# Token, norm, tap, subkey and bias layouts made by the host, and a first dense tile fed in quarters

## What is computed

```python
xn = rmsnorm(x, norm1_w)              # x * rsqrt(mean(x*x) + eps) * w
proj = xn @ w_in                      # 1024 -> 3088 columns; 16 of them feed a gate
log_a = log_sigmoid(gr @ gla_w_alpha + gla_b_alpha) / 16
...
s = einsum('thpd,hpkd->thpk', q, subkeys)      # product keys, top 16 of each half
...
u = h @ w_up; u = conv3(u, taps) + bias        # per channel, causal
h = h + sigmoid(rmsnorm(h) @ w_gate) * (p @ w_proj)   # side input p, two layers
...
logits = q . k * scale + rel_bias[bucket(t - s)]      # -inf outside the band of 128
```

## Time and profile before

| | us |
|---|---|
| median of 3 runs | 1544.4 |
| lowest, highest | 1544.03, 1548.16 |
| the profiled execution, its time | 1549.62 |
| the profiled execution, its span | 1547.8 |
| PE busy | 1387.3 (90%) |
| DVE busy | 1032.8 (67%) |
| ACT busy | 707.7 (46%) |
| POOL busy | 622.3 (40%) |

### The profile page before, as it was taken

How to read it: one execution, slowest core, us unless ns; L and a number is a source line. 1 busy time by engine, 2 the same in 40 slices (tenths; PEclk the granted TensorE clock), 3 DMA queues, 4 the chain that set the end, 5 groups by cost and what they waited for, 6 DMA issues and landing times.

```text
span 1547.8 us, 18260 instructions
## 1 busy us (share of the span) xinstructions
PE 1387.3 (90%) x5985; PEld 971.1 (63%) x5985; DVE 1032.8 (67%) x1923; ACT 707.7 (46%) x1374; POOL 622.3 (40%) x581
## 2 busy tenths in 40 slices
PE   7989979777787877787779999999999999999998
PEld 6877964333333333233335879788888788888887
DVE  5895787666666666666663548569863586498733
ACT  5534633233322333333334373477654745776534
POOL 2330777433333433333362521045442612364414
PEclk9999989999999999989999999899999999999999
DMA  9286699999999999999999500557665443476650
GB/s 319 82 143 224 217 333 411 421 422 421 422 423 421 421 422 422 422 421 422 422 413 348 200 29 35 164 163 210 196 211 178 159 142 108 121 207 194 216 193 28
DMA packets 187077, 415.00 MB, mean 268 GB/s; under 512 B 9883, under 2 KB 113923, under 8 KB 160387
## 3 DMA queue, kind: packets, MB, share of 16 engines
q0 software_dynamic: 43776, 268.45, 42.3%
q1 hardware_dynamic: 143090, 145.66, 30.6%
q10 hardware_dynamic: 144, 0.04, 0.0%
HBM read 409.93 MB, written 4.19 MB: 268 GB/s over the span
## 4 chain that ended last, share of the span: by engine, by line
PE 51%; DMA 21%; DVE 9%; POOL 7%; ACT 6%; issue 5%; ACTq 0%; POOLq 0%; DVEq 0%
DMA expert_rows<-in_peer_uv,route_idx 15%; PE ps L2548 10%; PE ps L2379 9%; PE ps L2092 7%; PE ps L2094 7%; PE ps L2093 7%; DMA scratch<-in_peer_uv,route_idx 5%; PE ps L2549 5%; DVE weights_lo L443 2%; POOL weights_lo L591 2%; POOL expert_rows L642 2%; ACT weights_hi L436 1%; POOL expert_rows L674 1%; PE ps L2057 1%; POOL expert_rows L661 1%
## 5 line engine op out<-in xcount | busy, mean ns | idle before, releaser
L1672 DVE CUSTOM_DVE_ANT_0 expert_rows<-expert_rows,ps 128x1024 f32<-128x1024 f32 x184 | 224.1, 1220 | 142.6 <-DMA expert_rows<-in_peer_uv,route_idx 131.6
L591 POOL TENSOR_TENSOR weights_lo<-weights_raw,weights_hi 128x512 fp32r<-128x512 f32 x120 | 159.6, 1366 | 374.5 <-ACT weights_hi L436 332.5
L2379 PE MATMUL ps<-expert_rows,scratch 128*128 128x512 f32 x512 | 241.9, 629 | 58.3 <-ACT scratch L981 58.3
L674 POOL DMA_INDIRECT expert_rows<-in_peer_uv,route_idx x156 | 148.3, 951 | 229.7 <-PE ps L2379 193.4
L436 ACT CAST weights_hi<-weights_raw 128x2048 fp32r<-128x2048 f32 x98 | 185.5, 1917 | 105.5 <-PE ps L2094 80.3
L2379 PEld LDWEIGHTS ps<-expert_rows,scratch 128*128 128x128 f32 x512 | 100.6, 201 | 198.6 <-issue 118.9
L2548 PE MATMUL ps<-x_normT,weights_hi 128*128 128x512 f32 x640 | 222.5, 393 | 0.0
L443 DVE TENSOR_TENSOR weights_lo<-weights_raw,weights_hi 128x2048 fp32r<-128x2048 f32 x68 | 160.5, 2366 | 74.4 <-ACT weights_hi L436 74.1
L967 ACT ACTIVATE proj<-proj 128x4 f32<-128x4 f32 x64 | 13.2, 206 | 402.1 <-DVE proj L1672 402.1
L2092 PE MATMUL ps<-weights_hi,x_normT 128*128 128x512 f32 (+1 forms) x496 | 188.1, 379 | 9.9 <-DVE weights_lo L443 4.2
L2094 PE MATMUL ps<-weights_hi,x_normT 128*128 128x512 f32 (+1 forms) x496 | 184.8, 372 | 0.0
(11 more groups left out here) (364 smaller groups left out, 2462.3 us busy)
## 6 DMA issues: line engine op xcount, KB each, us to landing
weights_raw<-in_ffn_up SPq DMA_DIRECT2D x88, 512.0 KB, 5.0
weights_raw<-in_ffn_down SPq DMA_DIRECT2D x22, 1024.0 KB, 4.9
weights_raw<-in_ab_w_in SPq DMA_DIRECT2D x14, 1024.0 KB, 5.7
weights_raw<-in_w_in SPq DMA_DIRECT2D x12, 1024.0 KB, 7.5
weights_raw<-in_ple_gate SPq DMA_DIRECT2D x8, 1024.0 KB, 6.2
weights_raw<-in_c_w_in SPq DMA_DIRECT2D x6, 1024.0 KB, 6.0
weights_raw<-in_w_out SPq DMA_DIRECT2D x4, 1024.0 KB, 12.7
weights_raw<-in_peer_w_query SPq DMA_DIRECT2D x4, 1024.0 KB, 12.4
```

The costliest lines, as they stand in the source:

```text
L591: ins = pool.tensor_tensor(w.lo[:, c], w.raw[:, c], w.hi[:, c].bitcast(F32), ALU.subtract)
L674: nc.gpsimd.indirect_dma_start(out=dst, out_offset=None, in_=table, in_offset=bass.IndirectOffsetOnAxis(ap=r_idx[:, q, n:n + 1], axis=0)). ...
L1672: ins = nc.vector.tensor_tensor_reduce(out=rows, in0=rows, in1=tokens, scale=1.0, scalar=0.0, op0=ALU.mult, op1=ALU.add, accum_out=r_dot[: ...
L2379: ins = pe.matmul(PS[:, (J[f"peer_{t}"] + m) % 8, :], DIAG[b][:, k, :], rows[:, m * BANK:(m + 1) * BANK], start=False, stop=False, skip_gr ...
```

## The change

- The host lays out x with the width on the partitions (`x_cols`), the six norm vectors as columns, taps and their bias as columns, the subkeys turned, the side input turned, and the banded bias in full (`window_bias`, 2 MB). The joined expert table was made by the host before, too.
- x in columns is loaded first, in two halves, then pieces 0 and 1, then x in rows. ACT and DVE make hi and lo of x from it, 8 instructions of 128x256 each.
- Pieces 0 and 1 are converted in quarters of 512 columns on ACT and DVE, and PE's first tile waits for each quarter by itself.
- The roots come behind these on ACT. The alpha job takes two banks. PE's turns, the eight spins, the conv and bias jobs, and the subkey and side-input jobs are gone from `PLAN`.
- One semaphore of the second block's gate is merged into another.

```diff
-PLAN = [("vecs", 1), ("norm0_0", 2), ("norm0_1", 2), ("win", 2), ("gr", 1), ("conv", 1), ("relb", 1),
-        ("win_1", 1), ("alpha", 1), ("win_1b", 1), ("win_2", 2), ...
+PLAN = [("win", 2), ("gr", 1),
+        ("win_1", 1), ("alpha", 2), ("win_1b", 1), ("win_2", 2), ...
...
+        "x_cols": inputs["x"][0].T.reshape(KC, P, S).transpose(1, 0, 2),
+        "vec_cols": np.concatenate([columns(n) for n in norms], 1),
+        "subkey_cols": inputs["peer_subkeys"][0].reshape(2 * PH, NKEYS, P).transpose(2, 0, 1),
+        "p_cols": inputs["p_2"][:, 0].transpose(0, 2, 1).reshape(2, 2, P, S).transpose(0, 2, 1, 3),
+        "window_bias": biases[rows].transpose(0, 2, 1),
...
@@ SP
-            sp.dma_start(C[:, 0:P], a["c_small"][:, 0:P]).then_inc(sem("ident_loaded"), 16)
-            for t in range(TT):
-                sp.dma_start(X[:, t, :], a["x"][0, t * P:(t + 1) * P, :]).then_inc(sem(f"x_loaded{t}"), 16)
+            for half in range(2):
+                cols = slice(4 * half, 4 * half + 4)
+                sp.dma_start(XCOLS[:, cols, :], a["x_cols"][:, cols, :]).then_inc(sem(f"x_cols_loaded{half}"), 16)
             for p in halves(0):
                 load("win", p)
+            for t in range(TT):
+                sp.dma_start(X[:, t, :], a["x"][0, t * P:(t + 1) * P, :]).then_inc(sem("x_loaded"), 16)
...
-            sp.wait_ge(evac_done, END["relb"])
-            sp.dma_start(bias_scratch.rearrange("h (t u) -> h t u", u=PER),
-                         BROW[:, 0:PER].unsqueeze(1).broadcast_to([SWH, P, PER])).then_inc(sem("bias_written"), 16)
...
-            sp.dma_start(SKN, a["peer_subkeys"][0].rearrange("h q k d -> k (h q) d")).then_inc(sem("subkeys_loaded"), 16)
-            sp.wait_ge(pe_done, END["subk_rest"])
...
+            sp.dma_start(BIAS, a["window_bias"]).then_inc(sem("bias_loaded"), 16)
@@ ACT
+            act.dma_start(VEC[:, :], a["vec_cols"]).then_inc(sem("vec_loaded"), 16)
...
+            for f in range(KC):
+                if f % 4 == 0:
+                    act.wait_ge(sem(f"x_cols_loaded{f // 4}"), 16)
+                nc.scalar.activation(XHI[:, f, :], XCOLS[:, f, :], ACT.Copy,
+                                     scale=VEC[:, NORM_COL[0] + f:NORM_COL[0] + f + 1]).then_inc(sem("first_hi"), 1)
+            for half in halves(0):
+                w = pieces["win", half]
+                act.wait_ge(raw_loaded[w.r], w.landed)
+                for c in range(4):
+                    cols = slice(c * BANK, (c + 1) * BANK)
+                    act.copy(w.hi[:, cols], w.raw[:, cols]).then_inc(hi_ready[w.h] if c == 3 else sem("first_hi"), 1)
             for t in range(TT):
-                norm_root(0, t, (sem(f"x_loaded{t}"), 16), (sem(f"x_loaded{t}"), 16))
-            act.wait_ge(evac_done, END["vecs"])
-            for half in range(2):
-                norm_hi(0, 0, (half,))
-                split("win", half)
-            norm_hi(0, 1)
+                norm_root(0, t, (sem("x_loaded"), 32), (sem("x_loaded"), 32))
@@ DVE
+            for half in halves(0):
+                w = pieces["win", half]
+                for c in range(4):
+                    cols = slice(c * BANK, (c + 1) * BANK)
+                    v.wait_ge(*((hi_ready[w.h], w.count) if c == 3 else (sem("first_hi"), KC + 3 * half + c + 1)))
+                    nc.vector.tensor_tensor(w.lo[:, cols], w.raw[:, cols], w.hi[:, cols].bitcast(F32),
+                                            ALU.subtract).then_inc(lo_ready[w.h] if c == 3 else sem("first_lo"), 1)
...
-            j = J["subk"]
-            freed(nc.vector.tensor_copy(SKT[:, 0:4, :], bank(j).rearrange("p (b t) -> p b t", b=4)), j)
@@ PE
-            for t in range(TT):
-                norm_T(0, t)
-            spin(J["win"], 8, P)
-            for t in range(TT):
-                dense_tile("win", 0, t, normed(0, t))
+            b = bank(tile_job("win", 0, 0))
+            for f in range(KC):
+                w, c = pieces["win", f // 4], f % 4
+                pe.wait_ge(*((lo_ready[w.h], w.count) if c == 3 else (sem("first_lo"), KC + 3 * (f // 4) + c + 1)))
+                hi, lo = part(w.hi, 4), part(w.lo, 4)
+                ins = product(b, xs(f, slice(0, P)), (hi[:, c, :], lo[:, c, :]), f == 0, f == KC - 1)
+            ins.then_inc(pe_done, 1)
+            dense_tile("win", 0, 1)
```

More of the change, by code:

```diff
@@ L1367, in _ @@
             v.wait_ge(sem("norm_rstd"), rstd_no[0])
-            for half in range(2):
-                norm_lo(0, 0, (half,))
-                split_lo(v, "win", half)
-            norm_lo(0, 1)
             v.wait_ge(sem("gr_hi_ready"), 1)
@@ L1377, in early_tables @@
                 freed(nc.vector.tensor_copy(GRT, bank(J["gr"])[0:GRANK, 0:S]), J["gr"])
-                freed(nc.vector.tensor_copy(CONV[:, :, :], bank(J["conv"])[:, 0:8 * 2 * FT].rearrange("p (l n) -> p l n", l=2)),
-                      J["conv"])
-                v.wait_ge(sem("rel_loaded"), 48)
-                freed(nc.vector.tensor_tensor(BROW, bank(J["relb"])[0:SWH, 0:384], OUTSIDE, ALU.add), J["relb"], wait=True)
                 v.wait_ge(sem("const_loaded"), 16)
@@ L2167, in _ @@
             ins.then_inc(pe_done, 1)
[L2168 to L2173 removed]
             dense_tile("win", 1, 0)
             pe.wait_ge(evac_done, END["gr"])
[L2176 removed]
             for t in range(TT):
[L2178 to L2179 removed]
+                pe.matmul(bank(J["alpha"] + t)[:, 0:256], GRT[:, t * P:(t + 1) * P], W_ALPHA,
+                          start=True, stop=True).then_inc(pe_done, 1)
             dense_tile("win", 1, 1)
@@ L2296, in _ @@
             spin(J["wout"], 3)
-            def subkeys(j, m):
-                pe.wait_ge(sem("subkeys_loaded"), 16)
-                transposes(j, [SKN[:, 4 * m + n, :] for n in range(4)])
             def head_tokens(t, j):
@@ L2319, in first_head @@
             def first_head():
-                subkeys(J["subk"], 0)
                 head_tokens(0, J["score_first"])
@@ L2329, in _ @@
             ins.then_inc(pe_done, 1)
-            for m in range(3):
-                subkeys(J["subk_rest"] + m, m + 1)
             head_tokens(1, J["query_0"])
```

127 lines of the change are left out of this document (48 added, 79 removed), and 4 rows, old and new, of the table PLAN.

## The result

| | us |
|---|---|
| kernel before, median of 22 runs | 1547.54 (1543.98 to 1552.63) |
| changed kernel, median of 22 runs | 1550.69 (1547.07 to 1555.46) |
| ratio of the two, 95% interval | 1.0020 (1.0012 to 1.0027) |
| profiled execution of the changed kernel: time, span | 1552.2, 1550.4 |

I had forecast 2.0 us less and measured about 3.1 us more. That lies inside the 0.3% that I had called no change, but its interval leaves out 1, and the forecast time and range are both missed. Of the 8.3 us between the forecast of 1542.4 and the 1550.7 measured, 3.1 are the starting point: I had counted from 1544.4, the median of three runs, and 22 runs gave 1547.5.

A forecast was written before the change was run, and what follows sets the result against it. The bound changes from stage to stage; at the start POOL's lo of piece 3 decides. The start's 2.0 us, all other edits zero, came off the median 1544.4: 1542.4 us, range 1537.5 to 1547.0.

The forecast's parts named there:

- The start sum: From first loads to the first `win_1` tile: done at 34.0 instead of 36.0 us, 2.0 us won.
- POOL's gap: Inside `win_1`, PE stands 2.4 us until POOL finishes the lo of piece 3 at 31.1 us.
- the cover behind it: Behind `win_1`: pieces 4 and 5 come no later, are wanted at 41 us, and the 2.0 us won stay.
- The subkeys' zero: At the subkey transposes: they are hidden in waits for DVE, so removing them wins zero.
- the covers gone: At the subkeys: 0.7 us instead of zero if the waits that hide the transposes and DVE's copy go.
- the rule on the clock: On PE: 1.2 GHz is the default and activity releases it; at the start real matmuls now pay for the warm-up.
- The side input's zero: At the side input's 4 transposes: PE waits 0.34 us for DVE anyway, so zero, at most 0.45 for each layer.
- the bias: Window bias transfers: no engine waits for them, so zero, with bounds 0 and 0.5 us.
- the banks: Second feed-forward: one of four pairs now straddles the last bank and is copied in two; zero.
- the tables' place: Tables in memory: another place named as an example of unseen effects, which together had 3%; no size given.
- Rival D: At the start: PE's clock stays at 1.2 GHz through both first tiles and `gr`; 5.9 us later, 1550.3; 4%.

The follow-up runs named there:

- kernels 9 and 10: Changed kernel repeated, 1.0025 to the kernel before; and the changed kernel with DVE's gate ahead of its lo passes of pieces 4 and 5, 0.9991.
- kernel 3: Kernel before with one wait on SP, so that pieces 4 and 5 are issued only after PE's gate-rank job; 1.0014 to the kernel before.
- kernel 11: Changed kernel with the gate ahead on DVE and the start's transfers and casts in the order they are wanted; 0.9970 to the kernel before, median 1541.5 us.
- kernels 15 and 16: Changed kernel with start rebuilt and gate ahead, side input turned by PE again, 0.9975 to the kernel before; the same with subkeys turned by PE too, 0.9979.
- kernel 2: Changed kernel with DVE's lo passes of pieces 4 and 5 moved behind the gate; 1.0017 to the kernel before.
- kernel 18: Start rebuilt, gate ahead, side input turned by PE, plus twelve spin matmuls ahead of the second head's tokens; 1.0021 to the kernel before, median 1555.7 us.
- third and fourth comparison: Two groups of follow-up runs, each on one chip against the kernel before, which took 1546.5 us in the third and 1545.4 in the fourth.
- fourth and fifth comparison: Two groups of follow-up runs on the same chip, against the kernel before, which took 1545.4 us in the fourth and 1552.4 in the fifth.
- kernel 1: Changed kernel with the loads of pieces 4 and 5 ahead of the small loads and DVE's wait for gains moved to the gate; 1.0034 to the kernel before.

## Why the prediction was wrong

**The start sum was right**: columns, casts, first matmul at 10.2, rise of the clock after 12 slow matmuls, POOL's gap, 2.8 us won at `win_1` against 2.0.

**The step that failed first** is the sentence on the cover behind it: "pieces 4 and 5 ... come behind one more megabyte but eight fewer issues on SP's queue, so no later, and are wanted at 41". They were issued 0.5 us earlier than before (the issues are seven fewer by the trace, not eight, since the columns take two), and landed 14.8 and 17.8 us after their issue. I had taken the time of issue for the time of landing, with no sum over what the transfer queue still held: one megabyte more, which I had myself put at 2.7 to 3.0 us, and the same eight small broadcast loads. The casts of the two pieces came 4.8 and 5.6 us later than in the kernel before. And "wanted at 41" was PE's want. On DVE the gate stands behind those passes in program order; I had not asked what is queued behind the waiting instruction there. The order costs 6.0 us by the medians of kernels 9 and 10, 4.7 by their means (one comparison), more than the 2.8 that the start had won; the two traces show 2.8 of it ahead of the gathers, just what the start had won. That kernel 3 lost only 2.5 us by the same late pieces, of the 4 to 7 expected, bounds how far this size carries over.

**The subkeys' zero** failed in its reason. They were hidden, and the 0.7 that I gave for "the covers gone" was the wrong price: what went with the 12 transposes was PE's clock, 1.5 us in the executions where it fell. I had weighed the rule on the clock for the start alone. The Trainium skill ("TensorE: Matmul & The Clock Gate", What's actually happening) says that activity releases the throttled state and that it is the default; the traces agree at this place too, 0.21 against 0.12 us between the same matmuls.

**The side input's zero** was too low: 0.55 us in the last layer, 1.1 in both by the two stretches, where I had at most 0.45 for each. I had counted the transposes that go and not where the operand of the remaining subtraction would lie.

**Right**, as far as it could be told: the bias (0.9999, with an interval of 0.002 to either side), the banks (the two feed-forwards take 110.4 to 110.6 us in every trace, from the first to the last use of the taps on DVE), the tables' place (0.9993).

**Rival D** had the sign, with the wrong mechanism; "such as another place of the tables" was the wrong unseen thing. A fifth rival, late pieces through DVE's order, could have been had from the rows.

**Open.** By the medians, 6.0 + 1.5 + 1.1 less the start's gain is more than 3.1 us, unless the start alone is worth 5.5; kernel 11 allows that (5.0 gained in spite of 2.6 for the two later parts), kernels 15 and 16 speak against it. By the traces, the start's gain and the order cancel (2.8 and 2.8), and 1.1 for the side input and 1.1 for the subkeys make 2.2 of the 3.1 us; the rest would be PE's clock behind the wait in `win_3`. That second sum is an estimate from a few traces, and no run tests it.

The kernel before took 1545.4 and 1546.5 us in the two comparisons in which kernels with the gate ahead were faster than it or level (0.9970 to 0.9991). Where it took 1556.9 and 1552.4, kernel 2, the same as kernel 10, came out at 1.0017, and kernel 18, which is kernel 15 with twelve spins, at 1.0021, though their traces show the first gathers as early as ever. From the 41st gather to the last takes 581 to 584 us in the ten traces of the first measurement and of the third and fourth comparison, and 586 to 593 in the ten others. The chip alone does not decide it, since the fourth and fifth comparison ran on one chip. That this stage (all gathers together move 268 MB) takes back what is won ahead of it is a guess, and not every trace bears it out: kernel 2 reaches the 41st gather 5.2 us ahead of kernel 3, on the same chip, and the last one still 4.2 us ahead. It is not settled, and so the version of kernel 11 beats both kernels in one comparison and not for certain everywhere.

## What to carry to other kernels

When a load moves behind others, sum up the bytes and packets ahead of it until it lands, and then look not at who wants it last but at what is queued behind the first instruction that waits for it. Before taking away work on PE that is hidden in a wait, look at the spacing of the matmuls behind that wait: the work may have been what kept the clock up. Before taking away a copy through PSUM, look at who else reads SBUF beside the instruction that then reads from there.

## What had not been expected of the hardware

- A load of 1 MB landed 17.8 us after its issue behind eight broadcast loads of 64 to 1024 bytes for each partition. While these were served the core's DMA moved 33 to 97 GB/s for some 6 us, against mostly 380 to 410 around that stretch. The kernel before has the same eight loads, and its rate falls too, 2 to 3 us earlier and for less long. The first 40 us, one figure for each microsecond, of the kernel before and of the changed kernel:

```profile
GB/s 0 31 157 305 388 401 395 408 404 381 366 251 371 387 387 387 396 403 356 209 130 32 15 81 337 400 420 383 399 389 387 387 389 383 387 387 389 389 381 387
...
GB/s 0 66 184 327 407 381 418 397 401 387 408 410 406 244 351 389 387 385 388 418 393 284 33 56 33 82 97 89 144 342 406 403 414 401 375 385 373 358 342 317
```

Issued ahead of these loads, in kernel 1, the two pieces landed 10.4 and 12.8 us after their issue. Why the low stretch is longer in the changed kernel is not shown.

- The issue of a 16x256 load on SP's queue took 5.14 us in the changed kernel, at 4.63 behind the gate-rank load, 4.21 in the kernel before at the same place in the order, and 0.44 in kernel 11, at 13.52, where the two token loads ahead of it took 5.58 instead.
- A 128x512 subtraction on DVE took 0.69 us with one operand in PSUM and 1.67 with both in SBUF, POOL at work beside it in either case; a quarter of a piece on POOL took 1.29 us alone and 3.31 beside a DVE pass that reads two tensors in SBUF.
- PE's start-to-start distance of 1.86 us at the second head's tokens was followed by 1.2 GHz in eight of eleven traces with the host's subkeys and no spins, the 0.54 us with the transposes in none of seven.
